# Output transposes by 64 rows ahead of the cross scores, in the last stage of a two-layer encoder step

## The reference

```
p = rmsnorm(x) @ w_in[l]         -> mixer inputs a, b, c (768 each) | cross query (256) | gate (1024)
layer 0: o = banded softmax attention (12 heads of 64, chunks of 64, 8 past chunks, distance bias)
layer 1: o = rmsnorm per head of a gated linear recurrence (6 heads, state 128 x 128)
both:    c = 4-head cross-attention into 256 memory tokens
y = concat(o, c) * silu(gate);   x = x + y @ w_out[l]
```

## Time and profile before

| what | value |
|---|---|
| median of 3 runs | 2380.48 us (2380.42 to 2388.09) |
| span of the profiled execution | 2376.1 us; its own time is not listed apart from the runs' |
| PE, DVE, ACT, POOL busy in the span | 97%, 77%, 59%, 16% |
| instructions | 61711 |
| stretch of the changed loop, 1966 to 2352 us | PE busy 379.44, DVE 314.91, ACT 252.05, POOL 77.63 of 386.00 us |
| granted PE clock in that stretch | 1.00 |

### The profile page before, as it was taken

How to read it: one execution, slowest core, us unless ns; L and a number is a source line. 1 busy time by engine, 2 the same in 40 slices (tenths; PEclk the granted TensorE clock), 3 DMA queues, 4 the chain that set the end, 5 groups by cost and what they waited for, 6 DMA issues and landing times. The chain is left out here.

```text
span 2376.1 us, 61711 instructions
## 1 busy us (share of the span) xinstructions
PE 2312.2 (97%) x23787; PEld 2094.7 (88%) x23787; DVE 1819.5 (77%) x3555; ACT 1413.5 (59%) x3281; POOL 381.0 (16%) x585
## 2 busy tenths in 40 slices
PE   7999999999989999999999999999999989999998
PEld 4999999999967888888887999999999978888886
DVE  7889788887666656666666998797888777888885
ACT  4564666755565555555554564776757566666664
POOL 2332000000022221211112332000000112112111
PEclk9999999999999999999999999999999999999999
DMA  6886887769894222222226897886879793444442
GB/s 227 298 299 219 301 281 231 247 220 332 232 307 121 83 66 89 90 69 83 73 81 232 272 303 242 256 275 214 266 248 312 230 269 117 129 131 122 137 135 70
DMA packets 396664, 469.64 MB, mean 198 GB/s; under 512 B 39860, under 2 KB 248556, under 8 KB 396376
## 3 DMA queue, kind: packets, MB, share of 16 engines
q1 hardware_dynamic: 379832, 406.02, 54.4%
q0 software_dynamic: 14704, 54.92, 6.6%
q10 hardware_dynamic: 1840, 4.75, 0.7%
HBM read 318.77 MB, written 151.56 MB: 198 GB/s over the span
## 5 line engine op out<-in xcount | busy, mean ns | idle before, releaser
L1468 PE MATMUL pj_acc<-x_lo,pj_wh 128*128 128x256 f32 (+1 forms) x3080 | 780.9, 284 | 0.0
L1468 PE MATMUL pj_acc<-x_hi,pj_wh 128*128 128x256 f32 (+1 forms) x3080 | 780.8, 284 | 0.0
L1468 PEld LDWEIGHTS pj_acc<-x_hi,pj_wh 128*128 128x128 f32 x3080 | 578.4, 188 | 0.0
L1468 PEld LDWEIGHTS pj_acc<-x_lo,pj_wh 128*128 128x128 f32 x3080 | 578.4, 188 | 0.0
L509 ACT ACTIVATE pj_wh<-pj_wt 128x512 fp32r<-128x512 f32 x676 | 420.3, 634 | 255.9 <-DMA pj_wt<-tsum 175.1
L516 DVE SCALAR_TENSOR_TENSOR pj_wl<-pj_wt,pj_wh 128x512 fp32r<-128x512 f32 x676 | 467.0, 708 | 87.0 <-ACT pj_wh L509 79.3
L1464 PE MATMUL pj_acc<-x_hi,pj_wl 128*128 128x256 f32 (+1 forms) x3080 | 509.4, 287 | 13.8 <-DVE pj_wl L516 11.9
L1464 PEld LDWEIGHTS pj_acc<-x_hi,pj_wl 128*128 128x128 f32 x3080 | 425.3, 188 | 22.1 <-DVE pj_wl L516 19.5
L1307 DVE TENSOR_TENSOR pj_out<-pj_out,pj_acc 128x512 f32<-128x512 f32 (+1 forms) x448 | 320.8, 716 | 103.3 <-PE pj_acc L1468 69.7
L2541 DVE COPY pb_pt<-pb_SCTP 128x256 f32<-128x256 f32 (+2 forms) x266 | 115.8, 435 | 147.5 <-PE pb_SCTP L2352 74.3
L2676 ACT ACTIVATE pb_se<-pb_se,pb_mn 128x640 f32<-128x640 f32 (+4 forms) x208 | 154.6, 745 | 114.6 <-DVE pb_mn L2524 114.3
(11 more groups left out here) (371 smaller groups left out, 3992.1 us busy)
## 6 DMA issues: line engine op xcount, KB each, us to landing
pj_wt<-tsum SPq DMA_DIRECT2D x546, 256.0 KB, 3.8
proj<-pj_out SPq DMA_DIRECT2D x112, 512.0 KB, 4.2
tsum<-pj_wt SPq DMA_DIRECT2D x140, 256.0 KB, 3.2
pj_wraw<-in_w_in_dram POOLq DMA_DIRECT2D x24, 1024.0 KB, 6.6
tsum<-pj_wraw SPq DMA_DIRECT2D x56, 256.0 KB, 4.2
hg_x<-x_mid SPq DMA_DIRECT2D x17, 512.0 KB, 3.7
pb_gate<-proj SPq DMA_DIRECT2D x16, 512.0 KB, 5.1
pb_x<-in_x_prompt_dram SPq DMA_DIRECT2D x16, 512.0 KB, 3.8
```

Source lines behind the costliest of these rows:

```text
L1468: ins = nc.tensor.matmul(BANK[j][:, 0:n], w.hi[j][:, k], x.of(y, p, j)[:, k], start=False, stop=(k == 3 and i == 1))
```

## The change

In tiles 1 to 15, PE no longer transposes the two halves of `o` ahead of and between the projection chunks 13 to 15. All three chunks come first, then `turn_outputs_rows` transposes all six heads, each as two pieces of 64 tokens x 128 columns, in turn on the two row halves of the array; then come the cross scores. Results of the first 64 tokens go to one bank of `TP`, of the other 64 to the second bank, so the gates read both banks with a new pattern. On DVE mask step 2 and the second half of the residual add come ahead of gate 0, gate 1 directly behind it, and then both low parts. Job 0 and job 16 stay as they were.

```diff
+                def turn_outputs_rows(job):
+
+                    pe.wait_ge(s_o, 2 * job)
+                    pe.wait_ge(s_ia, job + 1)
+                    pe.wait_ge(s_id, job + 1)
+                    for h in range(MG):
+                        for half in range(2):
+                            rows, at = slice(half * HD, (half + 1) * HD), 512 * half + h * HD
+                            ins = nc.tensor.transpose(TP[:, at:at + HD], o[rows, h * P:(h + 1) * P], ident[rows, rows])
+                    ins.then_inc(s_ot, 2)
+
...
                     level(t, 2)
                     if t:
-                        turn_outputs(t, 0)
-                        project(t - 1, LATE + 2, LATE + 4)
-                        turn_outputs(t, 1)
-                        project(t - 1, LATE + 4, CHUNKS)
+                        project(t - 1, LATE + 2, CHUNKS)
+                        turn_outputs_rows(t)
                     cross_scores(t)
                     level(t, 3)
                     project(t, 0, 3)
...
-                    nc.vector.tensor_tensor(y[c][:, 0:384], TP[:, 512 * c:512 * c + 384], g[:, 0:384], ALU.mult)
+                    if job < NT:
+                        turned = TP[:].rearrange("p (t x) -> p t x", t=2)[:, :, H3 * HD * c:H3 * HD * (c + 1)]
+                        nc.vector.tensor_tensor(y[c][:, 0:384].rearrange("p (i t n) -> p i t n", t=2, n=HD),
+                                                turned.rearrange("p t (i n) -> p i t n", n=HD),
+                                                g[:, 0:384].rearrange("p (i t n) -> p i t n", t=2, n=HD), ALU.mult)
+                    else:
+                        nc.vector.tensor_tensor(y[c][:, 0:384], TP[:, 512 * c:512 * c + 384], g[:, 0:384], ALU.mult)
...
                     place(t, 0)
                     place(t, 1)
+                    place(t, 2)
                     if t:
+                        add(t - 1, 1)
                         gate(t, 0)
-                    place(t, 2)
+                        gate(t, 1)
                     low_part(t, 0)
-                    if t:
-                        gate(t, 1)
-                        add(t - 1, 1)
                     low_part(t, 1)
```

## The result

Six runs of the changed kernel have a median of 2394.99 us (2386.76 to 2401.34), six of the kernel before 2381.15 (2379.99 to 2388.09). The ratio is 1.0045 [1.0029, 1.0062]: the change costs 10.7 us, with an interval from 6.9 to 14.8. The forecast was 2394.4, which is +13.9. The profiled execution took 2395.41, its span 2393.7.

A forecast was written before the change was run, and what follows sets the result against it. PE's own list bounds a tile unless a wait opens. Late gates hold the update 1.10 us in six tiles, 0.92 in nine: 14.9, less 1.0 issue waits, +13.9 on 2380.5 gives 2394.4; range 2389 to 2400, chance 0.55.

The forecast's parts named there:

- A: Time in a tile when level 2 is through; before the change the output transposes start there, 2147.47 in tile 8.
- 1.16 as a limit: At the first state update: its bank is free 1.16 us after the exponentials start, so PE waits until then.
- The rival that PE's list decides: 1.16 is chance, PE is never held at the update, only its list counts: 2376 us, faster by 4.8; chance 0.07.
- Row transposes, 0.65: On PE before the cross scores: twelve half-row transposes as six pairs of 0.11, 0.65 us; bounds 0.3 and 1.3.
- The rival of loads in turn: Row halves don't overlap, the twelve transposes take 1.3 us, the chain moves another 0.65 a tile: 2404 us; chance 0.13.
- Gate 0 at A+3.25: On DVE: gate 0 waits for the last row transpose, until A+3.25 instead of A+0.59; the add's floor is A+3.06.
- G: Start of gate 0 after the change, forecast at A+3.25; exponentials follow at G+3.43, the first update at G+4.59.
- Queues, pattern: SP's gate load and those behind it go 0.2 later; a gate stays at 0.67 us, bound 0.3 more each.
- Small wait at the third matmul: Next projection's third matmul on PE waits 0.22 us for low part 0, inside the larger wait at the update.
- Given back: Rival: issue waits of 3.1 us go, and cheap transposes drop gate 0 to the add's floor, 2.9: 2388 us; chance 0.23.
- Issue waits swallowed, 1.0: PE's issue waits in L2991, 1.1 us in three places, mostly vanish inside the new wait: 1.0 us less.
- The 4.4 around the span: Span 2376.1 against the runs' median 2380.5: the 4.4 us between were put down to what lies around the span.

The follow-up runs named there:

- the spare subtraction: Kernel before plus one unused 128x512 DVE subtraction between the second low part and the minima, tiles 1 to 15: period 26.21 against 25.76; 2381.78 us.
- the early exponentials: Changed kernel with the first minimum ahead of low part 1 and ACT's final square behind the exponentials: 2385.6 us against 2378.0, ratio 1.0024.
- the changed kernel with the later update: Changed kernel with both state updates one projection chunk later on PE: 2388.87 us against 2380.38, ratio 1.0030; mean period 26.30.

## Why the prediction was right

The mechanism is the one forecast: the gates wait, the minima and exponentials come late, and the update is held 1.16 behind them. That late minima are enough was shown by the spare subtraction. That the wait carries the cost is shown by where the loss lies (between A and the update, in every kernel whose update waits) and by the early exponentials, which bring that stretch back to 7.02. The whole time was not recovered in any run with the new place of the transposes, since issue waits behind the update take a share back. Point by point:

- **1.16 as a limit**: held, in all 15 tiles, and again in all 15 with the spare subtraction. The rival that PE's list decides falls. In the kernel before it is 1.16 or 1.17 in eight of the nine tiles that waited, 1.20 in the other.
- **Row transposes, 0.65**: mis-sized. The twelve took 0.42 (2134.07 to 2134.49), nearer to the lower bound of 0.3, and the cross scores start at A+2.71, not A+2.96. The rival of loads in turn falls. By the rule of the Trainium skill ("TensorE: Matmul & The Clock Gate", "LDWEIGHTS (loading the stationary operand)") that a load costs by its columns, even two side by side would have made an estimated 0.64; the measurement decides against it for this shape.
- **Gate 0 at A+3.25**: for that reason it falls to the floor that the add sets, forecast at A+3.06 and measured at A+3.00. So the gates wait for PE's third chunk, through the add, and not for the last row transpose, as the prediction had it. It is a close thing: by the prediction's own 0.29 the transposes (cross scores at A+2.71) would let gate 0 start at A+3.00 too. From there the chain runs as worked out: exponential at G+3.43 (2138.21 - 2134.78), update at A+7.59 instead of A+7.84. So the term per tile was 0.25 too large, 3.7 us in 15 tiles: 13.9 - 3.7 = 10.2, against the loop's measured 10.
- **Queues, pattern**: SP's gate load goes out at A+4.44, before A+4.48; I had expected 0.2 later. A gate still takes 0.67 (2134.78 to 2135.45) with the new pattern, as I chose; the bound of 0.3 each did not come.
- **Small wait at the third matmul**: there, in ten tiles (3.7 us at the load of L3058), inside the larger one.
- **Given back**: its arithmetic, 8 us, is also inside the interval, and its half about the add's floor came true. Its other half did not: PE's issue waits did not go (4.6 us after, 3.9 before), and they grow in the changed kernel when the wait is taken away, to 6.9 and 11.3.
- **Issue waits swallowed, 1.0**: held. In the kernel before, waits of L2991 ahead of the update (0.28 and 0.57) made tiles 4 and 13 take 7.18 and 7.50 up to it instead of 6.74, 1.2 together. In the changed kernel such waits are still there, 0.28 to 0.56 in tiles 4 to 6, and the update comes at A+7.59 to A+7.61 all the same.
- **What would show it**: the update behind the exponential and the idle ahead of the add are there. The minima come 1.03 later against A, not 1.1 to 1.3, and the period is 26.43, not 26.7, both because gate 0 comes 0.25 earlier.
- **The 4.4 around the span**: misread. The runs last 1.7 longer than their spans (2395.41 and 2393.7); the rest was scatter between executions. The forecast adds a difference to a median, so nothing hangs on it.

Forecast and median agree to 0.6 us, and such closeness is luck: of the +13.8 between the medians the loop explains 10, and the rest is within the scatter of the stretch before it. The interval, 6.9 to 14.8, holds both, and the rival's 8 as well, so it is the trace and not the time that tells them apart.

## What to carry to other kernels

Before two operations change places on a busy engine, follow the queue behind each of them to the next bank that the bound engine wants: here a transpose that got cheaper, and 0.24 us of PE saved, bought nothing, because the gates now stood behind an add. Look for a constant distance between a release and a start (1.16 or 1.17 in eight tiles of 15); where it repeats, the path runs through it, even if the profile names no releaser. And when a wait is removed, expect the next limit: two changed kernels without this wait gained less than their tiles' shortest periods promised.

## What the runs showed of the hardware

**Instruction supply.** PE's issue waits in this stage end 1.2 to 1.7 us after a packet of 16,384 bytes has landed on the DMA queue of instructions, in all twelve profiles, with two exceptions (2.0); where PE does not wait, its matmul at the same place of the grid starts about 3 to 4.5 behind the landing (medians, widely spread). From 1996 to 2350 us the changed kernel's queue starts 52 such packets and PE 6453 matmuls, one packet for 124. One such wait, in the changed kernel with the later update: 1.28 us, ended at 2032.30.

```profile
2032.30 0.83 PE L3001 MATMUL hg_SC<-hg_q,hg_k 128*32 128x64 f32 x22 [1.28 <-issue]
```
The DMA view of 2029 to 2033, in 40 slices (busy share in tenths, booked at the packet's start), and that queue's packets, MB and share of 16 engines:
```profile
DMA  0000008000000000000000000000000000000000
...
q8 instruction: 1, 0.02, 2.1%
```

The packet starts in the slice at 2029.6 and takes 2.1% of 16 engines x 4 us, 1.34 us; it has landed at about 2030.95, and PE goes on 1.35 later. With the grid of 125 matmuls this fits a list that comes in pieces: a PE that waits at a semaphore would let the next piece come in time, and one that doesn't would meet its end. No run shows this by itself, and why some pieces come late and others don't is not settled.

**Pairs on row halves.** Transposes of 64 rows x 128 columns went through at a pair each 0.07 us (0.42 for six pairs), against 0.125 each for those of whole rows (0.75 for six), both with the step to the cross scores.

**The clock.** A PE that stood for 0.35 and 1.64 us, nearly in a row, came back at the lower level, 1.2 GHz, for some microseconds (granted 0.66 on average from 2022 to 2027); after a single 1.56, in the changed kernel with the later update, the clock stayed at 1.00 and the spacing at 0.23. It is one case each.
